# Compressed values four heads at a time, and attention maxima subtracted by small diagonals beside the keys' remainder

## What is computed

```
o_cmp = softmax(q k_cmp^T) v_cmp        15 compressed keys for each group
o_slc = softmax(q k_sel^T) v_sel        causal, all 256 keys
o_win = softmax(q k_win^T) v_win        causal, all 256 keys
o     = gate0 * o_cmp + gate1 * o_slc + gate2 * o_win
x     = x + gate * ((o * silu(z)) @ w_out)
```

## Time and profile before

| | us |
|---|---|
| median of 3 runs | 892.94 (892.92 to 893.14) |
| profiled execution, its own time | 895.99 |
| span of its trace | 894.2 |
| TensorE busy | 868.4 |
| VectorE busy | 612.5 |
| ScalarE busy | 494.7 |
| GpSimd busy | 174.6 |

### The profile page before, as it was taken

One profiled execution on the slowest core, in us unless ns is written; L12 is line 12 of the kernel. 1 busy time (PEld: TensorE's weight loads), 2 busy tenths in 40 slices (PEclk: granted clock), 3 DMA queues, 4 the chain that ended last, 5 costly groups with the idle time before them and its releaser, 6 DMA issues.

```text
span 894.2 us, 14775 instructions
## 1 busy us (share of the span) xinstructions
PE 868.4 (97%) x5801; PEld 790.8 (88%) x5801; DVE 612.5 (68%) x976; ACT 494.7 (55%) x780; POOL 174.6 (20%) x189
## 2 busy tenths in 40 slices
PE   3899999999999999999999999999999999999998
PEld 3788899988688889999998888899999899999886
DVE  5875678877877687666665546597668666666552
ACT  3543768555657656544444546677765654444431
POOL 1016345565054520000000004271000000000000
PEclk9999999999999999999999999999999999999999
DMA  9966646456572665666666556553345566666650
GB/s 354 361 203 220 212 147 208 142 162 192 165 240 90 191 198 155 202 200 198 197 192 194 166 155 200 145 162 118 99 139 171 181 195 188 186 188 183 207 176 24
DMA packets 45844, 163.38 MB, mean 183 GB/s; under 512 B 5200, under 2 KB 5584, under 8 KB 45776
## 3 DMA queue, kind: packets, MB, share of 16 engines
q1 hardware_dynamic: 45776, 162.44, 57.4%
HBM read 161.37 MB, written 1.05 MB: 182 GB/s over the span
## 4 chain that ended last, share of the span: by engine, by line
PE 88%; DVE 5%; ACT 3%; DMA 2%; issue 1%; SPq 0%; POOL 0%; DVEq 0%; ACTq 0%
PE bank L518 36%; PE bank L506 34%; PE bank L533 3%; PE bank L703 2%; PE bank L865 2%; PE bank L680 2%; DVE w_lo L1673 1%; DMA x<-in_x 1%; PE bank L705 1%; PE bank L656 1%; DMA w_raw<-in_weights 1%; PE bank L613 1%; PE bank L684 1%; PE bank L759 1%; PE bank L707 1%
## 5 line engine op out<-in xcount | busy, mean ns | idle before, releaser
L1105 ACT ACTIVATE w_hi<-w_raw 128x1024 fp32r<-128x1024 f32 (+2 forms) x249 | 259.5, 1049 | 226.5 <-PE bank L518 121.1
L1673 DVE TENSOR_TENSOR w_lo<-w_raw,w_hi 128x1024 fp32r<-128x1024 f32 (+2 forms) x249 | 301.4, 1221 | 77.5 <-ACT w_hi L1105 76.9
L518 PE MATMUL bank<-h_hi,w_hi 128*128 128x256 f32 x904 | 254.6, 282 | 0.0
L518 PE MATMUL bank<-h_lo,w_hi 128*128 128x256 f32 x904 | 251.8, 279 | 0.0
L518 PE MATMUL bank<-h_hi,w_lo 128*128 128x256 f32 x904 | 251.8, 279 | 0.0
L518 PEld LDWEIGHTS bank<-h_lo,w_hi 128*128 128x128 f32 x904 | 171.4, 190 | 0.5 <-issue 0.2
L518 PEld LDWEIGHTS bank<-h_hi,w_hi 128*128 128x128 f32 x904 | 169.9, 188 | 1.0 <-issue 0.5
L518 PEld LDWEIGHTS bank<-h_hi,w_lo 128*128 128x128 f32 x904 | 169.8, 188 | 0.0
L506 PE MATMUL bank<-w_hi,h_hi 128*128 128x512 f32 (+1 forms) x240 | 96.5, 402 | 2.6 <-DVE w_lo L1673 1.9
L2548 POOL TENSOR_TENSOR ada_acc<-ada_acc,w_raw 128x512 f32<-128x512 f32 x56 | 82.2, 1468 | 68.3 <-ACT w_raw L1109 63.2
L506 PE MATMUL bank<-w_lo,h_hi 128*128 128x512 f32 (+1 forms) x240 | 94.0, 392 | 0.0
(11 more groups left out here) (321 smaller groups left out, 1404.5 us busy)
## 6 DMA issues: line engine op xcount, KB each, us to landing
w_raw<-in_weights SPq DMA_DIRECT2D x298, 512.0 KB, 4.3
w_raw<-in_weights SPq DMA_DIRECT2D x4, 360.0 KB, 3.6
x<-in_x SPq DMA_DIRECT2D x1, 1024.0 KB, 9.7
gate_row<-in_gate_bias SPq DMA_DIRECT2D x2, 512.0 KB, 6.9
out<-x SPq DMA_DIRECT2D x4, 256.0 KB, 3.4
w_raw<-in_weights SPq DMA_DIRECT2D x3, 256.0 KB, 2.6
const<-in_constants SPq DMA_DIRECT2D x1, 285.5 KB, 7.1
cols<-in_columns SPq DMA_DIRECT2D x1, 208.5 KB, 2.6
```

The lines of the kernel that those rows point to most:

```text
L518: mm = e.matmul(o, ws[p], xs[q], start=(k + kk == 0 and i == 0 and b % 2 == 0), stop=(k + kk == kts - 1 and i == 2 and (b % 2 == 1 or b == ...
L1105: e.activation(w_hi[i % NSPLIT][:, 0:c], raw[v % NRAW][:, 0:c], ACT.Copy).then_inc(*rounded(v))
L1673: e.tensor_tensor(w_lo[i % NSPLIT][:, 0:c], raw[v % NRAW][:, 0:c], w_hi[i % NSPLIT][:, 0:c].bitcast(F32), ALU.subtract).then_inc(*rested(v))
```

## The change

- `shifts`, `minus_r`, `shift` and `first_shifts` go. In their place `qm_first` (heads 0 to 3) and `qm` (heads 4 to 15, in the space of `h_hi` and `h_lo`, which are free once z1 is multiplied) hold the rounded queries in rows 0 to 63, copied there by DMA (`double`, three parts for each mixer), and maxima on small diagonals in rows 64 to 127.
- `spread_maxima` on VectorE writes these diagonals for four heads at a time. In the first mixer rows 64 to 95 belong to the selected keys and 96 to 127 to the window keys, with diagonals of 32: eight instructions of 32 rows by 256 elements. In the second mixer diagonals of 64: two instructions of 64 rows by 512.
- `kl` has the keys' remainder in rows 0 to 63 for all groups, and -1 in the rows 64 to 127 that belong to its keys, 0 in the others. The one product `kl` by `qm` gives the remainder's part and the subtraction. GpSimd fills these rows, and refills 32 of them between the mixers.
- `compressed_values` multiplies the compressed weights by the values of two groups at once, 128 columns, for four heads and two query tiles into bank 0: four products for each of four calls. VectorE multiplies the 512 columns by their factors (`compressed_weighed`) and adds them to `otok` (`compressed_added`), on which the turn now waits.
- `evict` has two parts for each head instead of three, and adds them with one instruction. The columns of conditioning chunks 6 and 7 go to bank 7 beside the values, and VectorE takes them over in `evict`.

Changed lines, each with the line before it where that helps, indented by eight less:

```diff
@@ -211,6 +211,9 @@
 ada = sb("ada", [P, 2, 3 * KT])
+doubles = ExitStack()
+qm = sb("qm", [P, NH, S], F32R, on=doubles)
+doubles.close()
@@ -267,14 +270,14 @@
 factors = sb("factors", [P, TT, 3, NH], on=mix)
-parts_of_o = sb("parts_of_o", [P, TT, 2, 3, HD], on=mix)
+parts_of_o = sb("parts_of_o", [P, TT, 2, 2, HD], on=mix)
...
 keys.close()
-shifts = [sb(f"shifts{x_}", [P, 2, TT, P], F32R, on=mix) for x_ in range(2)]
+qm_first = sb("qm_first", [P, 4, S], F32R, on=mix)
@@ -450,6 +454,10 @@
+def doubles_of(h):
+    return qm_first[:, h:4, :] if h < 4 else qm[:, h:NH, :]
@@ -672,17 +680,28 @@
         oa, ob = turned_items(x)
-        w.wait_ge(*(shift_done if i else shift_first).at((s, i, x)))
+        for at in (kl_signed.at(s), doubled[min(ha // 4, 2)].at((s, 1)), mx_spread.at((s, ha // 4))):
+            w.wait_ge(*at)
...
                 w.wait_ge(*at)
-            for m, k in enumerate((kh, kl)):
-                e.matmul(o, k[:, g, br, j * P:(j + 1) * P], qs[:, ha:hb + 1:2, j * P:S], start=m == 0, stop=False,
-                         skip_group_check=True)
+            for m, (k, q) in enumerate(((kh, qs[:, ha:hb + 1:2, j * P:S]),
+                                        (kl, doubles_of(ha)[:, 0:3:2, j * P:S]))):
+                e.matmul(o, k[:, g, br, j * P:(j + 1) * P], q, start=m == 0, stop=False, skip_group_check=True)
             e.matmul(o[:, :, 0:P], mask_r[:, :], bcast(unit_r[:, :].unsqueeze(1), [P, 2, P]), start=False,
-                     stop=False, skip_group_check=True)
-            e.matmul(o, minus_r[:, :], shifts[x][:, :, j:TT, :].rearrange("p a t q -> p a (t q)"), start=False,
...
+    def compressed_values(pr, free):
+        w.wait_ge(*zeroed.at(3))
+        w.wait_ge(*pc_done.at(1))
+        w.wait_ge(*free)
+        for t in range(TT):
+            for h in (4 * pr, 4 * pr + 2):
+                c0 = t * S + h % 4 * HD
+                mm = e.matmul(banks[0][:, c0:c0 + 2 * HD], pc_t[:, h // 2 % 4, t * P:(t + 1) * P],
+                              vc[:, group(h):group(h) + 2, :].rearrange("p g d -> p (g d)"), start=True, stop=True)
+        mm.then_inc(*comp_valued(pr))
@@ -703,12 +722,11 @@
                         mm = e.matmul(o, p[:, 2 * S + a * P:2 * S + (a + 1) * P], v[1], start=False, stop=True)
-                    if s == "nsa" and x == 1:
-                        mm = e.matmul(ov[t][:, a, 0, 0:HD], pc_t[:, h // 2 % 4, t * P:(t + 1) * P],
-                                      vc[:, group(h), :], start=True, stop=True)
...
         for i in range(n + 3):
+            if s == "nsa" and i == n:
+                compressed_values(3, o_gated.at(("nsa", 2)))
@@ -719,7 +737,7 @@
             if pr is not None:
-                w.wait_ge(*(o_summed.at((s, i - 2)) if s == "nsa" else o_gated.at((s, pr))))
+                w.wait_ge(*(comp_added.at(pr) if s == "nsa" else o_gated.at((s, pr))))
@@ -870,7 +888,9 @@
         if i == 1:
-            ada_columns(5, banks[0], pc_done.at(1))
+            compressed_values(0, pc_done.at(1))
+        if i == 2:
+            ada_columns(5, banks[0], comp_weighed.at(0))
@@ -879,15 +899,16 @@
         if i in (4, 6):
-            ada_columns(4 + i // 2, banks[0], o_gated.at(("nsa", i // 2 - 2)))
+            ada_columns(4 + i // 2, banks[7][:, 480:], o_evicted.at(("nsa", i - 1, 0)))
+            compressed_values(i // 2 - 1, o_gated.at(("nsa", i // 2 - 2)))
...
-    pair_attention("nsa", [v_done.at(("nsa", 1)), zeroed.at(3), pc_done.at(1)],
+    pair_attention("nsa", [v_done.at(("nsa", 1)), zeroed.at(3)],
                    [[[m_reduced.at(("nsa", 17)), c_masked.at(1)]] * 3, [m_reduced.at(("nsa", 17)), pc_done.at(0)],
-                    lambda pr: ada_cols.at(5 + min(pr, 2)) if pr else gate_row_done.at(5)], nsa_hook)
+                    lambda pr: comp_weighed.at(pr) if pr else gate_row_done.at(5)], nsa_hook)
@@ -1236,15 +1257,6 @@
-    def first_shifts(s):
-        for x_, it in enumerate(slots[s][0]["items"]):
-            w.wait_ge(*m_reduced.at(last_filling(s, it["heads"][1])))
-            for a, h in enumerate(it["heads"]):
-                for t in range(TT):
-                    last = copy(shifts[x_][:, a, t, :], ident, scale=mx_read[:, t, h, it["mx"]:it["mx"] + 1])
-            last.then_inc(*shift_first((s, 0, x_)))
@@ -1415,8 +1426,6 @@
         scale_chunk(5, j)
-        if j == 1:
-            first_shifts("nsa")
@@ -1499,8 +1508,6 @@
             z_half("moba_z0", 0, 1)
-        if j == 2:
-            first_shifts("moba")
@@ -1813,6 +1820,21 @@
+    def spread_maxima(s, g):
+        w.wait_ge(*m_reduced.at(last_filling(s, 4 * g + 3)))
+        if g:
+            w.wait_ge(*streamed.at((of[f"{s}_z1"][-1], 1)))
+        rows_ = 32 if s == "nsa" else 64
+        for i in range(P // rows_):
+            here = slice(rows_ * i, rows_ * i + rows_)
+            for br in range(2 if s == "nsa" else 1):
+                there = slice(HD + rows_ * br, HD + rows_ * br + rows_)
+                o = doubles_of(4 * g)[there, 0:4, :].rearrange("p h (t c) -> p t h c", t=TT)[:, :, :, here]
+                e.tensor_tensor(o, bcast(ident[here, here].unsqueeze(1).unsqueeze(1), [rows_, TT, 4, rows_]),
+                                bcast(mx_read[here, :, 4 * g:4 * g + 4, br].unsqueeze(3), [rows_, TT, 4, rows_]),
+                                ALU.mult).then_inc(*mx_spread((s, g)))
@@ -1821,26 +1843,26 @@
             if s == "nsa":
-                f = [factors[:, t, :, h:h + 3:2].rearrange("p b a -> p a b") for t in range(TT)]
+                f = [factors[:, t, 1:3, h:h + 3:2].rearrange("p b a -> p a b") for t in range(TT)]
                 g = gates[:, :, :].rearrange("p t (b h) -> p t b h", b=3)
+                if i in (4, 6):
+                    ada_column(4 + i // 2, banks[7][:, 480:])
                 for t in range(TT):
-                    step(e.reciprocal(f[t][:, :, 1:3], ov[t][:, :, 1:3, HD]))
+                    step(e.reciprocal(f[t], ov[t][:, :, :, HD]))
...
                 for t in range(TT):
-                    step(e.tensor_tensor(f[t][:, :, 1:3], f[t][:, :, 1:3],
-                                         g[:, t, 1:3, h:h + 3:2].rearrange("p b a -> p a b"), ALU.mult))
+                    step(e.tensor_tensor(f[t], f[t], g[:, t, 1:3, h:h + 3:2].rearrange("p b a -> p a b"), ALU.mult))
...
                     last = e.tensor_tensor(parts_of_o[:, t, :, :, :], ov[t][:, :, :, 0:HD],
-                                           bcast(f[t].unsqueeze(3), [P, 2, 3, HD]), ALU.mult)
+                                           bcast(f[t].unsqueeze(3), [P, 2, 2, HD]), ALU.mult)
...
                 w.wait_ge(*o_evicted.at((s, i)))
-                for t in range(TT):
-                    e.reduce_sum(otok[:, t, :].rearrange("p (h d) -> p h d", d=HD)[:, h:h + 3:2, :],
-                                 parts_of_o[:, t, :, :, :].rearrange("p a b d -> p a d b"),
-                                 AX.X).then_inc(*o_summed((s, i)))
+                e.tensor_tensor(otok[:, :, :].rearrange("p t (h d) -> p t h d", d=HD)[:, :, h:h + 3:2, :],
+                                parts_of_o[:, :, :, 0, :], parts_of_o[:, :, :, 1, :],
+                                ALU.add).then_inc(*o_summed((s, i)))
@@ -1851,22 +1873,34 @@
-        def shift(i, x_):
-            it = slots[s][i]["items"][x_]
-            (ha, hb), m = it["heads"], it["mx"]
-            w.wait_ge(*m_reduced.at(last_filling(s, hb)))
-            w.wait_ge(*scored.at((s, i - 1, x_, 1)))
-            e.tensor_tensor(shifts[x_][:, :, :, :], bcast(ident.unsqueeze(1).unsqueeze(1), [P, 2, TT, P]),
-                            bcast(mx_read[:, :, ha:hb + 1:2, m].rearrange("p t a -> p a t").unsqueeze(3),
-                                  [P, 2, TT, P]), ALU.mult).then_inc(*shift_done((s, i, x_)))
+        def compressed_weighed(pr):
+            w.wait_ge(*comp_valued.at(pr))
+            if pr:
+                w.wait_ge(*comp_added.at(pr - 1))
+            e.tensor_tensor(tmp[0][:, :].rearrange("p (t h d) -> p t h d", t=TT, h=4),
+                            banks[0][:, :].rearrange("p (t h d) -> p t h d", t=TT, h=4),
+                            bcast(factors[:, :, 0, 4 * pr:4 * pr + 4].unsqueeze(3), [P, TT, 4, HD]),
+                            ALU.mult).then_inc(*comp_weighed(pr))
+        def compressed_added(pr):
+            o = otok[:, :, pr * S:(pr + 1) * S]
+            w.wait_ge(*comp_weighed.at(pr))
+            w.wait_ge(*o_summed.at((s, 2 * pr + 1)))
+            e.tensor_tensor(o, o, tmp[0][:, :].rearrange("p (t n) -> p t n", t=TT),
+                            ALU.add).then_inc(*comp_added(pr))
...
             pr = slots[s][i - 2]["close"] if 0 <= i - 2 < n else None
+            if s == "nsa" and i == n:
+                compressed_weighed(3)
...
                 evict(i - 1)
-            for x_ in range(2 if i + 1 < n else 0):
-                shift(i + 1, x_)
+            if s == "nsa" and i in (0, 2, 4):
+                spread_maxima(s, i // 2 + 1)
```

(62 more changed lines are left out.)

## The result

The changed kernel takes 910.37 us (909.31 to 910.81, four runs), the kernel before 892.93 us (892.38 to 893.14, four runs beside them). The ratio is 1.019, 95% interval 1.0174 to 1.0206: 17.4 us slower, outside my range. The profiled execution of the changed kernel took 910.33 us with a span of 908.5.

A forecast was written before the change was run, and what follows sets the result against it. TensorE, busy 97% of the span, was taken as the bound. It would give up 11.9 us; after waits, 0.1 us (first attention) plus 0.9 (second) gained took 892.94 to 891.9, own range 890 to 894, 8-in-10 range 886.2 to 895.9.

The forecast's parts named there:

- What TensorE gives up: Both attentions: TensorE saves 11.9 us, 9.1 in the first and 2.8 in the second.
- rival 5: Compressed values: the 128-column products cost twice the 64-column ones, 3.5 us less gain, 895.4; chance 0.05.
- my signs of being wrong: First scores following at once, narrow products never above 0.5 us, or second attention's slot 1 waiting several us for a DMA.
- The wait of slot 1 on ScalarE: First attention: TensorE waits 0.9 us for slot 1's exponentials, behind ScalarE's tanh and scalings.
- the one before slot 4: First attention: late eviction 2 delays slot 4's exponential; a wait of 3.6 us, 3.2 of it new.
- the exclusive rule: VectorE's two-SBUF-input products and GpSimd's SBUF reads exclude each other: +3.4 us at both places, first attention loses 1.4.
- The start: Before the first turned scores: eight narrow products delay maxima 16 and 17 by 2.8 us, upper end 3.9 if w_lo meets a sum.
- The meeting with the sums: First attention, VectorE's iteration 2: four or five narrow products meet GpSimd's burst, +2.6 us, eviction 2 starts 3.6 us late.
- The wait in slot 5: First attention: the turn of slot 5 waits for the compressed addition and comes 2.3 us late (1.5 to 3.0).
- The second attention: Of 2.8 us freed, VectorE's lateness takes 1.1 and waiting for query copies 0.8; 0.9 us gained.
- rival 4: Second attention: query copies wait behind weight fetches at present times, 3.6 us instead of 0.8; 894.7; chance 0.10.
- Rival 3: First attention: VectorE becomes the bound, each two-input product meeting a burst waits for a whole sum; 895.8; chance 0.16.

The follow-up runs named there:

- d_wide: Changed kernel with two 64x512 products for four heads in the first attention too, leaving out one branch's maxima; 898.09 us.
- d_fill: Changed kernel with sixteen needless 512-column products in TensorE's wait before the first turned scores; 908.79 us.
- r1: Changed kernel with the first spread moved behind z0's last maxima, no longer ahead of maxima 16 and 17; 907.59 us.
- r_order: Changed kernel with the diagonals for heads 8 to 15 at the end of VectorE's iterations 2 and 4; 910.05 us.
- r_both: r_order with six ScalarE copies in place of the four DMAs of the second attention; 908.66 us.
- p_max: Kernel before with the diagonals, copies and signs, the compressed values as before; 906.48 us, ratio 1.015.
- p_comp: Kernel before with only the compressed values for four heads at a time and what belongs to them; 894.04 us, ratio 1.0014.
- a_nosum: Changed kernel with each of GpSimd's sums cut to 4 of 512 columns; 881.66 us.
- d_fill2: Changed kernel with sixteen needless 512-column products in TensorE's wait for the copies before slot 1 of the second attention; 910.91 us.
- v_comp5: p_comp with TensorE adding the compressed part for heads 12 to 15 while it turns, timed again; 892.13 us, ratio 0.9987 against the kernel before.
- a_nosum_copy: Changed kernel with GpSimd's sums cut and ScalarE's copies in place of the second attention's four DMAs; 885.44 us.
- v_moba: Kernel before with diagonals in the second attention alone, queries copied by ScalarE, first spread behind maxima of heads 4 to 7; 898.88 us, ratio 1.0074.

## Why the prediction was wrong, step by step

| stage | forecast | measured |
|---|---|---|
| z1 (start) | +2.8 | +5.0 |
| first attention behind it | -2.9 | +3.4 |
| between the attentions | 0 | +3.9 |
| second attention | -0.9 | +4.5 |

**What TensorE gives up** held. Eight compressed products start 0.81 us apart from what follows (160.59 to 161.40), so 0.10 each and 3.2 us for all where I had 3.6; rival 5 is out:

```profile
160.59 1.05 PE L702 MATMUL bank<-vc,zs 128*128 128x128 f32 x8
161.40 0.48 PE L662 MATMUL bank<-mask_r,unit_r 128*128 128x512 f32 x1
```

And d_wide shows 7.1 of the first attention's 9.1 us kept once VectorE's part is small.

**What I named as signs** came: the first scores late, products of 1.4 us beside sums, the wait of the slot-5 turn on the addition. So did one of my signs of being wrong, a DMA wait of 3.6 us in slot 1 of the second attention. The wait of slot 1 on ScalarE was 0.3 us where I had 0.9, and the one before slot 4 did not come. (My estimate of 1.4 us lost by the exclusive rule has a slip: 0.1 less twice 0.8 is 1.5 us lost.)

**The start: mis-sized.** I took 0.33 us for each narrow product, the pitch of the 128x256 pair in the earlier trace rows; it is 0.44, my upper bound, since the next starts only when the last is done. My rows were of products that keep the same partitions, one of them with an input in a bank; here every product writes another 32 rows than the one before. The Trainium skill (VectorE: DVE Perf Modes, Two Vector instructions with no wait between them) says just that: an instruction whose output or input starts in another group of 32 partitions than the last one's is held until all earlier ones have finished. I had not weighed it. The trace agrees: the products without a sum beside them start 0.45 us apart and are 0.42 long, and d_wide's pair, which changes only the rows of its inputs, starts 0.71 apart at 0.69. No run here had narrow products that stay in place, so that this is the reason is the page's word. The rest is the w_lo that I named as the upper end: 2.32 us instead of the 1.2 of a lone one. These two make 4.7 of the 5.0 us, above my upper end of 3.9.

**The meeting with the sums: right in size, wrong in place.** The forecast had +2.6 us for eight products, +3.4 if each waits for a whole sum. Measured are +2.9 and +3.9 (6.49 and 7.45 against 3.56), three and four products that each lose 1.0. But I followed the lateness through eviction 2, `gated` and ScalarE to slot 4. It strikes one slot sooner: the turn of slot 3 itself waits for the gate row (L1783), which stands behind the spread on VectorE. I had named that queue and not asked who waits for the gate row. The wait in slot 5 is the one I named, 3.3 us for a forecast of 2.3 (1.5 to 3.0). In all TensorE idles 6.8 us in the stage, 6.3 more than before, for a forecast of 6.4.

**The step that failed: a wait is not worth only its length.** My sum took each wait at its length and put the clock behind it at nothing. 9.1 us freed less 6.3 us of waits should have left the first attention 2.8 us shorter; it is 3.4 longer. Between them stands TensorE at 1.2 GHz behind three waits of 3.1 to 3.9 us: 13.7 us of its work there ran at half the clock, which is 6.9 us lost. With what the prediction says each version gives up the same sum comes out within 1 us in all of these, for the first attention against before (us; "clock" is half of the work done at 1.2 GHz):

| version | more waiting | clock | freed | sum | measured |
|---|---|---|---|---|---|
| after | 6.3 | 6.9 | 9.1 | +4.1 | +3.4 |
| d_fill | 6.1 | 3.3 | 9.1 | +0.3 | +1.2 |
| r1 | 3.8 | 5.0 | 9.1 | -0.3 | -0.1 |
| r_order | 5.9 | 8.5 | 9.1 | +5.3 | +4.4 |
| r_both | 6.9 | 3.3 | 9.1 | +1.1 | +0.9 |
| p_max | 4.1 | 4.8 | 5.6 | +3.3 | +3.1 |
| p_comp | 1.7 | 0 | 3.5 | -1.8 | -1.8 |
| d_wide | 1.7 | 0 | 9.1 | -7.4 | -7.1 |
| a_nosum | 1.2 | 0 | 9.1 | -7.9 | -7.6 |

Two runs took the clock by itself: d_fill gave back 2.1 us right behind one wait, d_fill2 1.6 us in the second attention. The Trainium skill (TensorE: Matmul & The Clock Gate, HAM oscillation — how this bites in real kernels) tells of this: idle gaps between bursts of matmuls throw the clock back to its lower level, and the next burst begins there. The traces agree in the main: in the changed kernel the clock fell during the wait or up to 0.6 us behind its end; in other versions it did not fall behind every wait of 1.8 to 2.7 us. Nothing in my text weighed it, although each of my waits (2.8, 3.2, 2.3) was near the length of those that set it off. In the kernel before these stages never leave 1.00, so no row of theirs could warn; the window from 40 to 60 us, at 0.91, could have: it holds a wait of 1.9 us for w_lo and 3.4 us at 1.2 GHz.

**Between the attentions: not in the forecast at all.** The 3.9 us are 2.2 of more waiting (the last turn 0.5, w_lo 1.6 where before had 0.8, maxima 0.8) and 3.4 us of work at 1.2 GHz, 1.7 lost, behind the first two. p_comp puts 2.8 us on the last added compressed values, which I had counted as 0.2 us gained, 1.2 of waiting and 1.7 of clock; v_comp5 took 2.2 of them back. p_max puts 1.7 there, without a fall of the clock. One cause on view is the first spread of the second attention, two products ahead of maxima 4 to 7, 3.37 us long beside sums where 1.41 is the lone price; TensorE waits 0.8 us for these maxima. I had looked at the second attention's spreads only inside it.

**The second attention: rival 4.** The copies were late by 3.6 us, the upper end that I had given a chance of 0.10, and the clock fell behind them. Of my assumption that weight fetches would be released 2.5 to 3 us sooner nothing can be seen: the copies were issued from 306.8 on, right behind z1's end at 305.9, and took longer than the fetches of the earlier trace rows:

```profile
L2710 SPq DMA_DIRECT2D qm<-qs x4: 596/704/962, 306.8 to 309.1; - x4
...
DMA to landing us min/median/max: 6.2/7.6/8.2
```

So they could not have been in time by their own length: TensorE stopped at 312.2, and 306.8 and 6.2 are 313.0. By the sum of above the stage has 3.5 of more waiting and 3.4 of clock against 2.8 freed, +4.1 for +4.5 measured. Without the copies and without sums it is no shorter than before (a_nosum_copy): the 2.8 us that TensorE gives up there go to waits for ScalarE's exponentials. With sums (v_moba) the wait for the diagonals and its clock come on top. I had kept 1.7 of them.

**Rival 3** had the mechanism: two-input products that wait for sums. It gave 2.9 us more than before; the change is 17.4 us slower with the sums and some 2 to 9 us faster without. Its chance of 0.16 was too low for a mechanism that the earlier trace rows already showed, and its sum left out what comes behind a long wait.

**What stays open.** p_comp and p_max sum to 14.2 of the 17.4 us: some 3 us come only with both together, which no run took apart, and p_max's executions lie 7 us apart. Why the clock fell behind one wait of 2.7 us and not behind another (r_order, r_both) is not shown, nor why it came back sooner in some places than in others. So the size of a wait's second price can't be forecast from these runs, only that there is one.

## What to carry to other kernels

When a change adds instructions to an engine that the bound engine waits for, count them one by one against the other user of a shared port, above all if they are small and many: with eight narrow products the first attention lost 3.4 us, with two wide ones of as many elements it kept 7 of the 9 us freed (in a kernel that leaves out one branch's maxima, and was still 4.7 us slower than before in all). Follow their lateness to every instruction queued behind them, and ask for each who waits. And give a wait of TensorE of the kind seen here (3.1 to 3.9 us) a second price for the work that then runs at half clock: 1.7 to 3.4 us behind each in the changed kernel, half of 3.4 to 6.8 us. Where the wait can't be removed, needless products in it held the clock, and gave back 2.1 and 1.6 us at the place. When you read a result, take the granted clock of each stretch, and add half of the work done at the lower one to the waits.

Compare stages between marks, not spans: two profiled executions with the same instructions differed by 3.3 us before the change had begun. Where long waits are in play even a stage differs by 1.3 us between executions of the same code (d_fill2 and after).

## What the runs showed of the hardware

- TensorE's granted clock fell from 2.4 to 1.2 GHz behind each idle stretch of 2.8 to 6.2 us in the two attentions, and came back 3 (p_max) to 12 us (r1, slot 3) after work had resumed. Behind shorter ones it fell in some places and not in others: it fell behind 0.5 and 1.6 us (after, 224.2 us), 1.9 (before, 44 us), 2.3 (v_moba) and 2.7 (r_order), not behind 1.8 (d_wide), 1.9 (d_fill, slot 5), 2.2 (d_fill2) and 2.7 (r_both). In r1 it fell after several short ones (busy 3.58 of 5 us from 135 us on): 143 to 146 us at 0.50.
- Beside GpSimd's sums a VectorE product of two SBUF tensors grew from 0.42 to 0.70 us on average (L1834), single ones from 0.42 to 1.4; one with an input from PSUM (L1859) stayed at 0.42, a reduction (L1821) at 0.68.
- Products of 32x256 that each write other partitions follow one another at 0.45 us (after, L1834), two of 128x256 that stay in place at 0.33.
- A copy of queries from SBUF to SBUF of 128 KB or 256 KB took 6.2 to 8.2 us from issue to landing beside weight fetches (after, 306.8 to 309.1 us).
